# Quad 5 of the MLPs' down projection moved from the plain to the seven-product form, in a two-layer decoder trunk

## What is computed

```python
D_MODEL, SEQ, D_FF = 2048, 256, 8192

def squared_relu_mlp(h, w_up, w_down):
    a = jnp.square(jax.nn.relu(h @ w_up))
    return a @ w_down

# per layer
    h = rmsnorm(x, ln_mlp_g[layer])
    x = x + squared_relu_mlp(h, mlp_w_up[layer], mlp_w_down[layer])
```

## Time and profile before

| | us |
|---|---|
| median of three runs (2057.89 to 2058.67) | 2058.46 |
| the profiled execution | 2057.91 |
| its span, first to last instruction | 2056.2 |
| PE busy | 2049.1 (100%) |
| PE weight load busy | 1757.1 (85%) |
| DVE busy | 1453.8 (71%) |
| ACT busy | 1109.3 (54%) |
| POOL busy | 217.2 (11%) |

### The profile page before, as it was taken

How to read it: one execution, slowest core, us unless ns; L and a number is a source line. 1 busy time by engine, 2 the same in 40 slices (tenths; PEclk the granted TensorE clock), 3 DMA queues, 4 the chain that set the end, 5 groups by cost and what they waited for, 6 DMA issues and landing times.

```text
span 2056.2 us, 26460 instructions
## 1 busy us (share of the span) xinstructions
PE 2049.1 (100%) x10488; PEld 1757.1 (85%) x10488; DVE 1453.8 (71%) x1967; ACT 1109.3 (54%) x1592; POOL 217.2 (11%) x317
## 2 busy tenths in 40 slices
PE   9999999999999999999999999999999999999999
PEld 8898888888888888888889888888888888888887
DVE  6556555566966877786696788557786696687777
ACT  6555565454644544554466786444554464454454
POOL 0000000020210120110010255001110021012010
PEclk9999999999999999999999999999999999999999
DMA  8555555585885795696576533568696588679565
GB/s 286 174 154 182 170 165 163 185 252 197 258 265 195 233 289 178 201 308 204 189 244 188 157 124 122 169 203 246 198 306 202 194 260 265 200 226 291 180 199 190
DMA packets 222195, 432.35 MB, mean 210 GB/s; under 512 B 12076, under 2 KB 26488, under 8 KB 222072
## 3 DMA queue, kind: packets, MB, share of 16 engines
q1 hardware_dynamic: 200520, 380.29, 55.6%
q0 software_dynamic: 21504, 50.34, 10.6%
q10 hardware_dynamic: 48, 0.02, 0.0%
HBM read 428.52 MB, written 2.10 MB: 209 GB/s over the span
## 4 chain that ended last, share of the span: by engine, by line
PE 98%; ACT 1%; DVE 1%; issue 0%; POOL 0%; POOLq 0%; DVEq 0%
PE psum L1592 23%; PE psum L1545 14%; PE psum L1547 14%; PE psum L1546 14%; PE psum L1595 12%; PE psum L1829 5%; PE psum L1828 5%; PE psum L1830 5%; PE psum L1674 1%; PE psum L1761 1%; PE psum L1616 1%; PE psum L1738 0%; PE psum L1762 0%; PE psum L1718 0%; PE psum L1719 0%; ACT nat L841 0%
## 5 line engine op out<-in xcount | busy, mean ns | idle before, releaser
L1078 DVE TENSOR_TENSOR halves<-raw,halves 128x1024 fp32r<-128x1024 f32 (+2 forms) x736 | 852.9, 1166 | 442.3 <-ACT halves L769 438.2
L769 ACT CAST halves<-raw 128x1024 fp32r<-128x1024 f32 (+2 forms) x736 | 728.3, 1001 | 593.3 <-PE psum L1547 298.6
L1592 PE MATMUL psum<-h,halves 128*128 128x512 f32 x2048 | 489.8, 391 | 0.0
L1592 PEld LDWEIGHTS psum<-h,halves 128*128 128x128 f32 x2048 | 376.4, 188 | 72.8
L1545 PE MATMUL psum<-halves,a 128*128 128x512 f32 x828 | 325.4, 393 | 0.3 <-ACT mix L836 0.3
L1547 PE MATMUL psum<-halves,a 128*128 128x512 f32 x828 | 322.6, 390 | 0.0
L1546 PE MATMUL psum<-halves,a 128*128 128x512 f32 x828 | 322.2, 389 | 0.0
L1595 PEld LDWEIGHTS psum<-h,halves 128*128 128x128 f32 x2048 | 262.7, 191 | 10.0
L1595 PE MATMUL psum<-h,halves 128*128 128x256 f32 x2048 | 266.1, 283 | 0.0
L1545 PE MATMUL psum<-halves,h 128*128 128x512 f32 (+4 forms) x572 | 213.4, 373 | 0.2 <-DVE h L1276 0.2
L1547 PE MATMUL psum<-halves,h 128*128 128x512 f32 (+4 forms) x572 | 206.9, 362 | 0.0
(11 more groups left out here) (265 smaller groups left out, 2083.8 us busy)
## 6 DMA issues: line engine op xcount, KB each, us to landing
raw<-in_mlp_w_up SPq DMA_DIRECT2D x128, 1024.0 KB, 6.1
raw<-in_mlp_w_down SPq DMA_DIRECT2D x128, 1024.0 KB, 5.2
mix<-in_mlp_w_down POOLq DMA_DIRECT2D x192, 256.0 KB, 7.1
raw<-in_sf_w_in SPq DMA_DIRECT2D x41, 1024.0 KB, 5.2
raw<-in_sf_w_o SPq DMA_DIRECT2D x16, 1024.0 KB, 5.2
raw<-in_mla_w_o SPq DMA_DIRECT2D x16, 1024.0 KB, 5.1
raw<-in_mla_w_ukv SPq DMA_DIRECT2D x8, 1024.0 KB, 5.5
raw<-in_sf_w_in SPq DMA_DIRECT2D x14, 512.0 KB, 3.9
```

The costliest lines, as they stand in the source:

```text
L769: nc.scalar.copy(half_piece(n, 0), raw_piece(n)).then_inc(hi_done, 1)
L1078: v.tensor_tensor(half_piece(n, 1), raw_piece(n), half_piece(n, 0).bitcast(F32), ALU.subtract)\
L1592: last = mm(bank, half_piece(n, 0)[:, cols], src[:, k].rearrange("p s t -> p (s t)"), start=(k == 0), stop=(k == KT - 1))
```

## The change

Quad 5 becomes a fast quad: a block has 7 fast quads and one plain one, quad 2. The pieces of a block go from 76 to 78, and `quad_at` becomes 40, 44, 48, 50, 54, 58, 62, 66, with chunk 3 at 70. The weight sums stand at j = 34, 37 and then five pieces ahead of each quad (45, 49, 53, 57, 61). The seventh pair of weight blocks takes the third `u_sum` buffer. Loads of the third chunk whose two quads are both fast (three of four per block) bring only the rows that are read, half a load. The token sums of the seventh quad need a place: those of quad 5 are made inside the last chunk of the up projection, the remaining ones keep the places behind it, and `sd_nat` gets a second half.

```diff
-FAST_QUADS = 0, 1, 3, 4, 6, 7
-PLAIN_QUADS = 2, 5
-U_BUFFER = 0, 1, 2, 3, 0, 1
+FAST_QUADS = 0, 1, 3, 4, 5, 6, 7
+PLAIN_QUADS = 2,
+U_BUFFER = 0, 1, 2, 3, 0, 1, 2
+FAST = len(FAST_QUADS)
...
-        with nc.sbuf_tensor("sd_nat", [P, 4, 2, P], F32R) as sd_nat:
+        with nc.sbuf_tensor("sd_nat", [P, 2, 4, 2, P], F32R) as sd_nat:
...
-                def fetch(load, src):
+                def fetch(load, src, second_rows=False):
                     free_slot(load)
-                    sp_.dma_start(raw[:, load % SLOTS].rearrange("p (k n) -> p k n", k=4),
-                                  src.rearrange("(k p) n -> p k n", p=P)).then_inc(raw_loaded[load % SLOTS], 16)
+                    dst, src = raw[:, load % SLOTS].rearrange("p (q k n) -> p q k n", q=2, k=2), \
+                        src.rearrange("(q k p) n -> p q k n", q=2, p=P)
+                    if second_rows:
+                        dst, src = dst[:, :, 1], src[:, :, 1]
+                    else:
+                        dst, src = dst.rearrange("p q k n -> p (q k) n"), src.rearrange("p q k n -> p (q k) n")
+                    sp_.dma_start(dst, src).then_inc(raw_loaded[load % SLOTS], 16)
...
-                    fetch(load, w_down[b0 * D + 4 * P * l:b0 * D + 4 * P * (l + 1), c * N:(c + 1) * N])
+
+                    both_fast = c == 2 and 2 * l in FAST_QUADS and 2 * l + 1 in FAST_QUADS
+                    fetch(load, w_down[b0 * D + 4 * P * l:b0 * D + 4 * P * (l + 1), c * N:(c + 1) * N], both_fast)
...
-                    for m in (0, 2, 4):
-                        u_load(layer, b0, m)
-                        u_load(layer, b0, m + 1)
-                        u_add(layer, b0, m)
-                        u_add(layer, b0, m + 1)
+                    for pair in ((0, 1), (2, 3), (4, 5), (6,)):
+                        for m in pair:
+                            u_load(layer, b0, m)
+                        for m in pair:
+                            u_add(layer, b0, m)
...
-                        if c == 1 and j == 3:
-                            token_sums_hi(no, 1)
+                        if c in (1, 3) and j == 3:
+                            token_sums_hi(no, (1, 4)[c // 2])
...
-                    token_sums_hi(no, c + 1 if c else 0)
+                    token_sums_hi(no, (0, 2, 3, 5)[c])
...
-                        if c == 1 and j == 2:
-                            token_sums(no, 1)
-                        if c == 1 and j == 4:
-                            token_sums_lo(no, 1)
+                        if c in (1, 3) and j == 2:
+                            token_sums(no, (1, 4)[c // 2])
+                        if c in (1, 3) and j == 4:
+                            token_sums_lo(no, (1, 4)[c // 2])
...
-                sums = {34: 0, 37: 1, quad_at(2) - 3: 2, quad_at(3) - 1: 3, quad_at(5) - 2: 4, quad_at(6) - 1: 5}
+                sums = {34: 0, 37: 1, **{quad_at(q) - 5: m for m, q in enumerate(FAST_QUADS) if m > 1}}
```

More of the change, by code:

```diff
@@ L135, in summed_count @@
 def summed_count(layer, b0, m):
-    return 32 * (3 * block_no(layer, b0) + m // 2 + 1)
+    return 32 * (len(FAST_QUADS[m % 2::2]) * block_no(layer, b0) + m // 2 + 1)
 def stepped_count(layer, b0, m):
-    return 2 * (6 * block_no(layer, b0) + m + 1)
+    return 2 * (FAST * block_no(layer, b0) + m + 1)
 def quad_at(q):
@@ L436, in sd_of @@
         def sd_of(i):
-            return sd[:, i] if i < 4 else (sd_last, sd_nat)[i - 4][:]
+            return sd[:, i] if i < 4 else sd_last[:] if i == 4 else sd_nat[:, i - 5]
         def out_on_pool(n):
@@ L1020, in token_sums_hi @@
             def token_sums_hi(no, i):
-                act.wait_ge(a_step, 24 * no + 4 * i + 4)
+                act.wait_ge(a_step, 4 * (FAST * no + i) + 4)
                 nc.scalar.copy(sd_of(i)[:, :, 0], a_sum).then_inc(sd_hi, 1)
@@ L1043, in mlp_block @@
                     if j == 34:
-                        token_sums_hi(no, 5)
-                    for at, slot, bank in ((quad_at(7) - 1, 3, X8), (quad_at(7), 0, X1)):
+                        token_sums_hi(no, 6)
+                    for at, slot, bank, m in ((quad_at(7) - 1, 3, X8, 3), (quad_at(7), 0, X1, 6)):
                         if j == at:
                             act.wait_ge(pieces_used, base + at + 1)
-                            act.wait_ge(lo_done, base + quad_at(FAST_QUADS[3]) + 2)
+                            act.wait_ge(lo_done, base + quad_at(FAST_QUADS[m]) + 2)
                             nc.scalar.copy(c_sum[:, slot], bank).then_inc(joint_copied, 1)
@@ L1395, in token_sums @@
             def token_sums(no, i):
-                done = 24 * no + 4 * i
+                done = 4 * (FAST * no + i)
                 if done:
@@ L1409, in token_sums_lo @@
             def token_sums_lo(no, i):
-                dve.wait_ge(sd_hi, 6 * no + i + 1)
+                dve.wait_ge(sd_hi, FAST * no + i + 1)
                 v.tensor_tensor(sd_of(i)[:, :, 1], a_sum, sd_of(i)[:, :, 0].bitcast(F32), ALU.subtract)                 .then_inc(sd_ready, 1)
@@ L1465, in mlp_block @@
                         if c and j == 1:
-                            token_sums_lo(no, c if c > 1 else 0)
-                        if c == 1 and j == 2:
-                            token_sums(no, 1)
-                        if c == 1 and j == 4:
-                            token_sums_lo(no, 1)
+                            token_sums_lo(no, (0, 2, 3)[c - 1])
+                        if c in (1, 3) and j == 2:
+                            token_sums(no, (1, 4)[c // 2])
+                        if c in (1, 3) and j == 4:
+                            token_sums_lo(no, (1, 4)[c // 2])
                         if b0 == 0 and c == 0 and j == 2:
@@ L1484, in mlp_block @@
                                     ALU.subtract).then_inc(split_done, 1)
-                    token_sums(no, c + 1 if c else 0)
-                sums = {34: 0, 37: 1, quad_at(2) - 3: 2, quad_at(3) - 1: 3, quad_at(5) - 2: 4, quad_at(6) - 1: 5}
+                    token_sums(no, (0, 2, 3, 5)[c])
+                sums = {34: 0, 37: 1, **{quad_at(q) - 5: m for m, q in enumerate(FAST_QUADS) if m > 1}}
                 end = quad_at(8)
@@ L1506, in mlp_block @@
                     if j == 33:
-                        token_sums_lo(no, 4)
-                        token_sums(no, 5)
+                        token_sums_lo(no, 5)
+                        token_sums(no, 6)
                     if j == 35:
-                        token_sums_lo(no, 5)
+                        token_sums_lo(no, 6)
                     if j in sums:
@@ L1891, in mlp_block @@
                             if q in FAST_QUADS:
-                                pe.wait_ge(sd_ready, 6 * no + FAST_QUADS.index(q) + 1)
+                                pe.wait_ge(sd_ready, FAST * no + FAST_QUADS.index(q) + 1)
                                 fast_quad(base + quad_at(q), q, added0 + 1)
```

## The result

| | before | after |
|---|---|---|
| median | 2058.27 us | 2074.74 us |
| lowest to highest | 2057.89 to 2058.67 us | 2072.44 to 2079.59 us |
| the profiled execution's own time | 2057.91 us | 2079.59 us |
| its span | 2056.2 us | 2077.9 us |

The ratio is 1.0083 (95% interval 1.0065 to 1.0101): 16.5 us slower, where the forecast had 7.9. The sign held, and the range of 2060 to 2072 us did not. The profiled execution of after is the slowest of its runs, and the spread (7 us against 0.8) is itself part of what has to be explained.

The account below looks back on a forecast made before the run. The prediction took PE's instruction stream as the bound (busy 2049.1 of 2056.2 us). From the profiled 2057.91 us it took 5.44, added 13.2 of stall for 2065.7, then 0.55 to the median: 2066.2 us, range 2060 to 2072.

Parts of the forecast that it names:

- PE's work: Quad 5 on PE: three matmuls fewer per block over 8 blocks, at 0.2267 us each, saving 5.44 us.
- The stall of quads 5 to 7: PE waits for DVE's low halves at these quads' first pieces: 1.65 us per block, 13.2 us in all.
- The round: DVE's work for one fast quad: 5.36 us against PE's 4.76, so DVE loses 0.60 us per fast quad.
- a block of 173.0 us: Sign of the forecast in the MLPs: block time 172.03 - 0.68 + 1.65 us.
- All hidden: Rival for quads 3 to 7: DVE keeps up and PE keeps its 5.44 us, giving 2053.0 us; chance 0.11.
- The seventh sum: Quad 7's loads and adds on POOL: landed by 717.9, DVE asks at 720.20, hidden with 2 us to spare.
- The seventh sum comes late: Rival: quad 7's loads and adds overrun the margin by 2 us per block, 16 us on top, 2082; chance 0.07.
- a restart: PE resuming after a wait for DVE: 0.25 us beyond the lateness, counted once per block, at most three times.
- the halved loads: Three of four third-chunk loads per block on SP, halved: worth nothing, since PE waited for no low half.
- ACT's additional halves: Two more high halves and a token-sum copy per block on ACT: covered, otherwise 3.2 us per block.
- the token sums of chunk 3: One more set on DVE in the up projection: hidden, otherwise 3.6 us per block.

Follow-up runs that it names:

- experiment 5: After without quad 7's plain loads and the second DVE weight sum of quads 5 to 7: 2052.65 us; same sum left out, those loads on SP: 2069.89 us.
- experiment 1: After without the two plain loads of quad 7's weight sums in each block: 2066.05 us.
- experiment 3: After with whole third-chunk loads again: 2071.88 us; before with the halved third-chunk loads alone: 2058.14 us.
- experiment 4: After with quad 6's adding loads cut to 8 columns: 2065.62 us; after with two halved raw loads per block cut to 64 columns: 2077.67 us.
- experiment 6: After with plain quad at place 4, narrow pieces' own buffer, quad 7's loads on SP: 2053.51 us; loads on POOL: 2060.65; without narrow buffer: 2063.94.

## Why the prediction came out as it did

**PE's work: right.** 24 matmuls fewer at 0.2267 us, 5.44 us. Where neither wait is left, the gain shows whole: 2052.65 in experiment 5, against 2058.00 before on its chip, is 5.35 us.

**The stall of quads 5 to 7: right, in place, cause and size.** The round was forecast as 5.36 and measured 5.33 to 5.34; 24 waits, at the first pieces of these quads, are what it named (the rows list most at 0.17 to 0.33 us, where it said 0.3 to 0.6); a block of 173.0 us is measured as 172.92 (experiment 1) and as 172.95 in the one block of after whose seventh sum isn't late. A block without a stall takes 172.03 - 0.68 = 171.35, so a stall of 1.6 us where 1.65 was forecast. The rows of waits alone would give only half of it (0.81 us in that block: 0.18, 0.30, 0.33). The idle time counts from the modelled end of the last matmul, 0.39 us after its start, although the next could have started after 0.23; this hides 0.16 per wait, and the restart (0.31 instead of 0.23) adds 0.08. 0.81 + 3 x 0.24 = 1.53.

**"All hidden": refuted by the same stage.** The Trainium skill, "Perfetto Trace Analysis", § Identifying the Most-Contended Engine, has one look for the engine with the highest occupancy, and judge TensorE by the busy share of its weight loads. The prediction took PE's matmul share instead. Both shares name PE (weight loads 84% here, matmuls 99%, against DVE's 71%), and yet taking work from PE made the kernel slower. In experiment 5 a sum less on DVE gave the gain back. What decides is the stage's rounds and the lead, and no share of the whole span shows either.

**The seventh sum: wrong, and this is the miss.** The step that failed is the one on POOL: the loads are issued and "land 5.8 us later at 707.6", so that the adds were "Hidden with 2 us to spare". The order of work was right: load behind quad 6's adds, adds behind the load, DVE behind the adds. The size of one term was not. The 5.8 us of the earlier trace rows was read from a plain load that goes out with no adds under way; the moved one goes out right behind two, and took 10.6 in block 1. The difference of 4.8 us is larger than the 2 us to spare. The kernel before had a sign of this: SP's 1 MB loads that go out beside POOL's adds (522.60 and 527.86 us in block 1) took 9.9 to 10.4 us there, twice the median of the earlier trace rows that the prediction used. The prediction moved the load past the adds on POOL and counted the wait for POOL to be free, but kept the landing time of the old place. With the bounds that the rows gave (5.8 for a plain load, up to 9.2 for an accumulating one), 9.2 would have brought the adds' landing to about 721.3, behind DVE's 720.20, and the rival "The seventh sum comes late" would have had more than 0.07. Its place and condition were right, its price (2 us in each block) too high: 8.9 us over seven blocks.

**The clock: not foreseen.** The prediction bounded a restart by 0.25 us per wait. Behind three of the waits that the late sum made longer, the lower clock cost 1.5 us more each; other runs had waits as long without that (last section). This and the changing lateness of the adds (from nothing to 2.2 us from block to block) would explain the spread of 7 us between runs, but one execution alone was traced, so that this is argued; in experiment 1, with neither, runs of the same kernel lie within 1.6 us (2065.28 to 2066.86).

**What was counted at nothing:** the halved loads are nothing (experiment 3). ACT's additional halves and the token sums of chunk 3 cost nothing either: a block has 172.95 us, with no room for the 3.2 or 3.6 us that they would cost uncovered.

## What to carry to other kernels

Where two engines alternate over buffers, compare their rounds in the stage that changes and count how many rounds the lead lasts: a run of short rounds can be broken up by a long one in its middle, or given a deeper buffer, and here the two, with an earlier load, turned 16.5 us lost into 4.5 won. When a transfer is moved, its landing time must be read from a transfer in the new company, not from the same transfer in its old place; where no such row exists, set the margin against the longest landing of the queue. Remove one suspect at a time, but look at what the removal lets arrive earlier: the shorter DVE round of experiment 5 waited 17.2 us for the load that had cost 5.2.

## What the runs showed of the hardware that was not expected

**Accumulating loads take more of the DMA engines for each byte, and hold up others.** The queues of before and of after (packets, MB, share of the 16 engines' span):

```profile
q1 hardware_dynamic: 200520, 380.29, 55.6%
q0 software_dynamic: 21504, 50.34, 10.6%
```

```profile
q1 hardware_dynamic: 194376, 367.71, 53.7%
q0 software_dynamic: 25088, 58.73, 12.4%
```

In after POOL's queue, plain and accumulating loads together, took 12.4 / 58.73 = 0.211% per MB, SP's 53.7 / 367.71 = 0.146: 1.45 times as much. A plain load beside two accumulating ones landed in 10.6 us from POOL's queue, 9.9 from SP's, and 7.2 with the accumulating ones cut to 8 columns. Two stretches of before in which POOL's queue carried one kind alone give the price: plain loads moved 0.52 MB in 512 to 519 us with 22.0% of the 16 engines, accumulating ones 0.79 MB in 528 to 537 us with 47.4%, which is 47 and 86 us of one engine's time per MB. Loads of SP's queue landed sooner too when the accumulating ones were cut (experiment 4).

**A wait of some 2 us on PE can be followed by the lower clock, and need not be.** In the traced execution of after, behind waits of 2.62, 2.09 and 2.48 us, seven or eight matmuls ran 0.43 us apart, with a granted clock of 0.50 to 0.51; behind 1.54 us and less they ran at full clock. The length of the wait alone doesn't decide. In experiment 3 (whole loads) a wait of 1.89 us was followed by the lower clock and one of 2.21 was not; in experiment 5 (one sum less, with quad 7's loads) 2.02 and 2.48 were and 2.33 was not; in experiment 6 (loads on POOL) 2.18 was not. What decides stays open.

**What else was in flight counted for more than a load's size.** In before, SP's loads of 1 MB landed in 5.2 us in the median and in 9.9 to 10.4 us beside POOL's adds, and halving the load at a given place took off 1.4 or 1.5 us (experiment 3).
